# A two-layer hybrid encoder on one core: column tiles placed around a two-way scan, and the convolution branch's norm issued at other places

## The chip, the cores and the metric

The kernel runs on one core of one Trainium2 chip. The metric is the device time of one execution in microseconds (us), lower is better. Five engines work side by side, each through its own list of instructions in order, and wait for each other on semaphores: TensorE (PE in the profile) multiplies matrices, VectorE (DVE) and GpSimd (POOL) do elementwise work, ScalarE (ACT) does functions of one input and roundings, SyncE (SP) issues the weight transfers.

## What is computed

Two layers, 256 tokens, width 1024, all in float32. In each, with the gated branches in the middle:

```python
x = x + 0.5 * swiglu(rms_norm(x, norm_ffn1[i]), ffn1_w1[i], ffn1_w3[i], ffn1_w2[i])
h = rms_norm(x, norm_mix[i])
proj = h @ w_in[i]
y_rw, v_first = rwkv7_branch(p_rw, h, ...)       # a delta-rule scan over time, in both directions
y_cv = conformer_conv_branch(p_cv, ...)          # 31 taps, layer norm, silu, @ cv_w_branch
y_mla = mla_branch(p_mla, ...)                   # attention
merged = gates[:, :, 0] * y_rw + gates[:, :, 1] * y_cv + gates[:, :, 2] * y_mla
x = x + merged @ w_o[i]
x = x + 0.5 * swiglu(rms_norm(x, norm_ffn2[i]), ffn2_w1[i], ffn2_w3[i], ffn2_w2[i])
```

The end of the scan branch is a group norm over each head's 64 channels, and a bonus term:

```python
o = layer_norm(o, gn_g.reshape(H, N), gn_b.reshape(H, N), RW_GN_EPS)
k_bonus = jnp.mean(k_dir, axis=2).reshape(B, S, H, N)
bonus = jnp.sum(rf.reshape(B, S, H, N) * k_bonus * r_k, axis=-1, keepdims=True) * vf.reshape(B, S, H, N)
o = (o + bonus).reshape(B, S, C).astype(h.dtype)
return (o * g) @ w_branch, v_first
```

The convolution branch normalises over its 512 channels: `jax.nn.silu(layer_norm(u, ln_g, ln_b, CV_LN_EPS))`.

## The kernel before

Activations lie transposed, channels on the 128 partitions and the 256 tokens along them. **Column tiles.** The weights come as a stream of 128x1024 tiles, three slots deep. ACT rounds a tile to its high part (`hi`, L1108), DVE takes the rest (`lo`, L1443), and PE makes three products of each 128x128 block (`products`, L545 to L547: high weight times high and low activation, low weight times high activation). Three such products are a **piece**, and eight pieces are a tile (`tile_pieces`) or the two output tiles of a branch (`branch_pieces`). SP may refill a slot once the low part is taken; ACT may round into it once PE has used the tile before.

**The scan stage** follows the attention. It runs twice (`for d in range(2)`), once per direction, as a chain that hops between PE and DVE: decays and directed keys on DVE (`decays`, `directed`, then the products with the keys, L1820 to L1828), transposes on PE ("tk", L915), pair products for two quads of heads (`("pairs", d, q)`, L927 to L937, masked by DVE in L1842 to L1859), five levels of inverting a 64x64 triangle ("z", L948, and "mz", L957 and L959, with a DVE step after each), outputs (L997 to L1003), states and the sum `osum`. Then come the group norm: mean (L1061), bonus sums (L1064), squares summed (L1072), the inverse spread over the heads (L1077), and its elementwise end on DVE.

**Filling.** While PE waits in that chain it shall do column tiles. The tables `FILL_A` and `FILL_R` say how many pieces PE does at each named point of the chain (`fr.at("values")` and so on; one object per engine walks the same points). `FILL_R` hands out 192 pieces: 96 of the attention branch (weights and gates, which need its `u`), then 96 of the convolution branch, written by hand as counts and in this order only. ACT and DVE do one unit of their part (round the next tile, gate, merge into `merged`) at a point for each whole eight pieces that PE will have been given by then, so the same table moves work on three engines. The banks 6 and 7 take these pieces in turn, and a branch piece waits until DVE has merged what its bank held (`("merge", b, c)`). The scan branch's own tiles (`branch_pieces(2, ...)`) come last, after the group norm; they begin with two gate tiles and then need `u` of the scan.

**The convolution branch's norm** is threaded through the change of direction: PE sums the channels (`"cv mean"`, L1011), ACT scales, POOL subtracts (L508), ACT squares (L1402), PE sums (`"cv var"`, L1043), ACT takes the root (L1408), DVE the reciprocal (L1921), POOL multiplies (L515), ACT gives sigmoid and weighted value (L1372, L1375), POOL multiplies them (L520), ACT rounds (L1379), POOL takes the rest (L526), and PE's first convolution piece waits for that.

## Time and profile before

| what | value |
| --- | --- |
| three runs before | 1731.34, 1732.7, 1738.39 us, median 1732.7 |
| the profiled execution | 1740.08 us |
| its span, first to last instruction | 1738.1 us |
| PE's mean granted clock in it | 0.964 of 2.4 GHz |
| PE busy | 93% of the span |
| DVE busy | 69% |
| ACT busy | 45% |

The span is one execution seen by the profiler; 2.0 us of its time lie around it. A PE that is busy for 93% is not a PE at its peak: matmul ends are modelled, and at the lower of its two clocks (1.2 instead of 2.4 GHz) the same matmul counts as busy for longer. So the time of a stage is read from where a matmul starts, what it waited for, and the granted clock there.

### The profile page before, as it was taken

Reading aid. Unit: us, or ns where it says so; the run is one execution under the profiler, and the core shown is the slowest. Engines: PE = TensorE matmul, PEld = TensorE weight load, DVE = VectorE, ACT = ScalarE, POOL = GpSimd, SP = SyncE. Lnnn points to the kernel's source line nnn. Section 1 sums busy time; section 2 is a strip of 40 time slices with the busy share of each in tenths; the row PEclk is TensorE's granted clock in tenths of the full one; section 3 lists DMA queues with packets and bytes.
Section 4 is the critical chain, followed back from the end, with each engine's and each line's share of the span. In section 5 each row is a group of like instructions: output and inputs, shape, how many; then the busy total and the mean of one; then the engine's idle time right before and its main releaser. Section 6 shows DMA issues by size and latency. Waiting matters only on the chain.

```text
span 1738.1 us, 43046 instructions
## 1 busy us (share of the span) xinstructions
PE 1608.8 (93%) x16861; PEld 1489.9 (86%) x16861; DVE 1203.0 (69%) x1784; ACT 778.3 (45%) x1195; POOL 94.7 (5%) x112
## 2 busy tenths in 40 slices
PE   6999999898978899999999999988999798999998
PEld 6999886778868789999889999867788686899997
DVE  4777675788675456777666786667887655667766
ACT  5444564472251245544444446534614412454444
POOL 1000020000020001000100002000000200010001
PEclk9999998999999999999999999989999898999999
DMA  5755531331021234555557555322311202445555
GB/s 184 270 183 183 182 122 61 98 100 61 27 74 39 87 102 161 190 182 181 191 182 243 182 185 175 103 74 85 110 39 39 82 21 85 144 151 195 182 183 193
DMA packets 62925, 231.55 MB, mean 133 GB/s; under 512 B 7024, under 2 KB 8048, under 8 KB 61840
## 3 DMA queue, kind: packets, MB, share of 16 engines
q1 hardware_dynamic: 61488, 221.41, 38.7%
q0 software_dynamic: 1248, 7.46, 1.2%
q8 instruction: 138, 2.26, 0.5%
q14 instruction: 51, 0.42, 0.1%
HBM read 228.09 MB, written 1.05 MB: 132 GB/s over the span
## 4 chain that ended last, share of the span: by engine, by line
PE 79%; DVE 8%; issue 6%; ACT 4%; DMA 3%; POOL 0%; DVEq 0%; ACTq 0%; SPq 0%; POOLq 0%
PE banks L545 16%; PE banks L546 15%; PE banks L547 15%; PE banks L612 9%; PE banks L613 5%; DMA raw<-in_stream 3%; PE banks L959 2%; PE banks L957 2%; DVE wlo L1443 2%; PE banks L948 1%; ACT whi L1108 1%; DVE arena L1882 1%; PE banks L837 1%; ACT arena L1286 1%; PE banks L723 1%
## 5 line engine op out<-in xcount | busy, mean ns | idle before, releaser
L1443 DVE TENSOR_TENSOR wlo<-raw,whi 128x1024 fp32r<-128x1024 f32 x417 | 511.5, 1230 | 302.0 <-ACT whi L1108 300.1
L1108 ACT CAST whi<-raw 128x1024 fp32r<-128x1024 f32 x417 | 436.3, 1050 | 456.4 <-PE banks L547 315.3
L545 PE MATMUL banks<-hx,whi 128*128 128x256 f32 x1696 | 489.6, 289 | 39.8 <-DVE wlo L1443 18.7
L546 PE MATMUL banks<-hx,whi 128*128 128x256 f32 x1696 | 485.1, 286 | 0.0
L547 PE MATMUL banks<-hx,wlo 128*128 128x256 f32 x1696 | 484.8, 286 | 0.0
L545 PEld LDWEIGHTS banks<-hx,whi 128*128 128x128 f32 x1696 | 330.6, 195 | 45.1 <-issue 32.3
L546 PEld LDWEIGHTS banks<-hx,whi 128*128 128x128 f32 x1696 | 330.8, 195 | 0.2
L547 PEld LDWEIGHTS banks<-hx,wlo 128*128 128x128 f32 x1696 | 330.7, 195 | 0.0
L545 PE MATMUL banks<-h,whi 128*128 128x256 f32 x896 | 272.4, 304 | 29.4 <-ACT arena L1206 17.6
L546 PE MATMUL banks<-h,whi 128*128 128x256 f32 x896 | 261.3, 292 | 0.0
L547 PE MATMUL banks<-h,wlo 128*128 128x256 f32 x896 | 260.4, 291 | 0.0
L612 PE MATMUL banks<-gg,whi 128*128 128x512 f32 x704 | 245.8, 393 | 0.0
L545 PEld LDWEIGHTS banks<-h,whi 128*128 128x128 f32 x896 | 180.0, 201 | 48.1 <-issue 32.4
L613 PE MATMUL banks<-gg,wlo 128*128 128x256 f32 x704 | 197.3, 280 | 0.0
L546 PEld LDWEIGHTS banks<-h,whi 128*128 128x128 f32 x896 | 180.1, 201 | 0.7 <-issue 0.5
L547 PEld LDWEIGHTS banks<-h,wlo 128*128 128x128 f32 x896 | 179.5, 200 | 0.0
L612 PEld LDWEIGHTS banks<-gg,whi 128*128 128x128 f32 x704 | 132.5, 188 | 30.3
L613 PEld LDWEIGHTS banks<-gg,wlo 128*128 128x128 f32 x704 | 131.8, 187 | 0.0
L1671 DVE SCALAR_TENSOR_TENSOR cvx<-arena,vec_t,cvx 128x256 f32<-128x256 f32 x240 | 99.0, 479 | 0.0
L959 PE MATMUL banks<-arena 64*64 64x64 f32 x1280 | 72.5, 220 | 0.1
L959 PEld LDWEIGHTS banks<-arena 64*64 64x64 f32 x1280 | 69.8, 137 | 0.2
L1385 ACT COPY arena<-banks 128x512 f32<-128x512 f32 x8 | 4.7, 586 | 141.8 <-PE banks L966 141.8
(291 smaller groups left out, 1869.3 us busy)
## 6 DMA issues: line engine op xcount, KB each, us to landing
raw<-in_stream SPq DMA_DIRECT2D x417, 512.0 KB, 3.4
arena<-in_wuq POOLq DMA_DIRECT2D x2, 1152.0 KB, 10.3
lo_w<-in_lora POOLq DMA_DIRECT2D x2, 1024.0 KB, 7.0
arena<-in_wukv POOLq DMA_DIRECT2D x2, 1024.0 KB, 13.5
xT<-in_x SPq DMA_DIRECT2D x1, 1024.0 KB, 5.0
out<-xT SPq DMA_DIRECT2D x8, 128.0 KB, 3.7
consts<-in_cst SPq DMA_DIRECT2D x1, 642.5 KB, 8.4
vec_t<-in_vecs POOLq DMA_DIRECT2D x3, 113.0 KB, 4.1
```

Of the source, the lines that this page charges most:

```text
L545: TE.matmul(o, wh, hi, start=first, stop=False, **kw)
L546: TE.matmul(o, wh, lo, start=False, stop=False, **kw)
L547: return TE.matmul(o, wl, hi, start=False, stop=last, **kw)
L612: TE.matmul(o[:, :], whi[:, slot, w], gg[:, j, :, :], start=j == 0, stop=False, skip_group_check=True)
L613: last = TE.matmul(o[:, 0:S], wlo[:, slot, w], gg[:, j, 0, :], start=False, stop=j == NFF - 1, skip_group_check=True)
L723: m = TE.matmul(bank[4 + j // 2][:, (j % 2) * S:(j % 2 + 1) * S], wuq[:, c, j * P:(j + 1) * P], lat[:, c, :], start=c == 0, stop=c == QC - 1)
L837: m = TE.matmul(bank[two_banks[c // 2]][:, (c % 2) * S:(c % 2 + 1) * S], lo_w[HD * d:HD * d + HD, col, c * P:(c + 1) * P], wag[HD * d:HD * ...
L957: TE.matmul(bank[3 * q + 1][e, o], mn[e, 1, 4 * q + x, t, :], zz[e, 4 * q + x, t, :], start=True, stop=True)
L959: m = TE.matmul(bank[3 * q + 2][e, o], zz[e, 4 * q + x, t, :], mn[e, 1, 4 * q + x, t, :], start=True, stop=True)
L1108: SE.copy(whi[:, m % HL, :], raw[:, m % RAW, :]).then_inc(hi_ready, 1)
L1443: TT(wlo[:, m % HL, :], raw[:, m % RAW, :], whi[:, m % HL, :].bitcast(F), ALU.subtract)\
L1671: m = STT(cvo[:, c, :], src, vv("cv_w", c * TAPS + t), cvo[:, c, :], ALU.mult, ALU.add)
```

## The change

The table gives other counts, and two new points: "sums over" after the last sum of the scan, with 8 pieces, and "gn sums" after the group norm's squares, with 12. The sum stays 192. "values" gets 13 for 5, and the second direction's points before its levels get fewer. Around it the order on the engines moves: "cv mean" comes later on PE, "cv var" sooner, ACT's squares and DVE's reciprocal sooner; the sigmoid of the normalised values goes ahead of ACT's copies of the transposes; the sum of the directed keys and the bonus terms go from DVE's chain into the levels 3 and 4 of the second direction; a copy of 16 elements (`wch`) goes from DVE to ACT; the bonus sums take banks 4 and 5, since 6 and 7 hold pieces now.

```diff
-FILL_R = {"key sums": 6, "decay": 8, "nu": 5, "values": 5}
+FILL_R = {"key sums": 6, "decay": 8, "nu": 5, "values": 13}
 for _d in range(2):
-    FILL_R.update({("kr", _d): (14, 16)[_d], ("tk", _d): (4, 6)[_d], ("pairs", _d, 0): (6, 20)[_d],
-                   ("pairs", _d, 1): (6, 20)[_d], ("x", _d): (4, 18)[_d], ("o", _d): (4, 14)[_d]})
-    FILL_R.update({("state", _d, i): n for i, n in enumerate(((4, 4, 4), (12, 6, 6))[_d])})
+    FILL_R.update({("kr", _d): (14, 10)[_d], ("tk", _d): (4, 4)[_d], ("pairs", _d, 0): (5, 12)[_d],
+                   ("pairs", _d, 1): (6, 10)[_d], ("x", _d): (4, 16)[_d], ("o", _d): (3, 15)[_d]})
+    FILL_R.update({("state", _d, i): n for i, n in enumerate(((4, 4, 4), (12, 7, 6))[_d])})
+FILL_R.update({"sums over": 8, "gn sums": 12})
...
                 local(d, 1)
-                if d == 0:
-                    pe.wait_ge(*vec.at(("conv", *CONV_TAPS[-1][::-1])))
-                    for c in range(RC):
-                        m = TE.matmul(bank[5][:, 0:S], cc("ones", P), cvo[:, c, :], start=c == 0, stop=c == RC - 1)
-                    m.then_inc(*ten.mark("cv mean"))
                 fr.at(("o", d))
...
                 local(d, 2)
                 if d == 0:
+                    pe.wait_ge(*vec.at(("conv", *CONV_TAPS[-1][::-1])))
+                    for c in range(RC):
+                        m = TE.matmul(bank[5][:, 0:S], cc("ones", P), cvo[:, c, :], start=c == 0, stop=c == RC - 1)
+                    m.then_inc(*ten.mark("cv mean"))
                     lora(1, 0, (1, 4))
...
                     if d == 0 and i == 1:
                         pe.wait_ge(*act.at(("sw", 1)))
                         lora(1, 1, (1, 4))
+                        pe.wait_ge(*act.at("cv squares"))
+                        for c in range(RC):
+                            m = TE.matmul(bank[5][:, 0:S], cc("ones", P), cv_sq[:, c, :], start=c == 0,
+                                          stop=c == RC - 1)
+                        m.then_inc(*ten.mark("cv var"))
                 fr.at(("state", d, 2))
-                if d == 0:
-                    pe.wait_ge(*act.at("cv squares"))
-                    pe.wait_ge(*vec.at(("qw", d, 0)))
-                    for c in range(RC):
-                        m = TE.matmul(bank[0][:, 0:S], cc("ones", P), cv_sq[:, c, :], start=c == 0, stop=c == RC - 1)
-                    m.then_inc(*ten.mark("cv var"))
...
+            fr.at("sums over")
             pe.wait_ge(*vec.at(("osum", 1)))
-            pe.wait_ge(*vec.at("bonus terms"))
             for b in range(2):
                 m = TE.matmul(bank[b][:, :], cc("mean64", P), osum[:, 2 * b:2 * b + 2, :], start=True, stop=True)
             m.then_inc(*ten.mark("gn mean"))
+            pe.wait_ge(*vec.at("bonus terms"))
             for b in range(2):
-                m = TE.matmul(bank[6 + b][:, :], cc("mean64", P), tA[:, 2 * b:2 * b + 2, :], start=True, stop=True)
+                m = TE.matmul(bank[4 + b][:, :], cc("mean64", P), kds[:, 2 * b:2 * b + 2, :], start=True, stop=True)
             m.then_inc(*ten.mark("bonus"))
...
-                m = TE.matmul(bank[4][0:H, 0:S], cc("es", H, j * SUMS), tB[:, j, :], start=j == 0, stop=j == RC - 1)
+                m = TE.matmul(bank[0][0:H, 0:S], cc("es", H, j * SUMS), tB[:, j, :], start=j == 0, stop=j == RC - 1)
             m.then_inc(*ten.mark("gn sums"))
+            fr.at("gn sums")
             pe.wait_ge(*vec.at("gn inverse"))
...
                 SE.activation(tC_, tC_, ACT.Exp, scale=DECAY).then_inc(*act.mark(("winv", d)))
+                if d:
+                    sc.wait_ge(*vec.at(("qw", 0, 2)))
+                edge = C - 1 if d == 0 else 0
+                SE.copy(wch, tA.rearrange("p c (n e) -> p c n e", e=C)[:, :, :, edge]).then_inc(*act.mark(("wch", d)))
                 SE.preload_act_table(ACT.Sigmoid)
...
                 fr.at(("kr", d))
+                if d:
+                    for c in range(RC):
+                        sc.wait_ge(*poo.at(("cv normed", c)))
+                        SE.activation(cv_sq[:, c, :], cvo[:, c, :], ACT.Sigmoid, bias=vv("ln_b", c), scale=vv("ln_g", c))\
+                            .then_inc(*act.mark(("cv sigmoid", c)))
+                        if c % 2:
+                            for i in (c - 1, c):
+                                sc.wait_ge(*act.at(("cv sigmoid", i)))
+                                SE.activation(cvo[:, i, :], cvo[:, i, :], ACT.Identity, bias=vv("ln_b", i),
+                                              scale=vv("ln_g", i)).then_inc(*act.mark(("cv weighted", i)))
                 for q in range(6):
                     sc.wait_ge(*ten.at(("tk", d, q)))
                     SE.copy(tk[:, q // NT, q % NT, :], bank[q][:, :]).then_inc(*act.mark(("tk", d, q)))
                 fr.at(("tk", d))
                 if d:
-                    for c in range(RC):
...
                 fr.at(("x", d))
+                fr.at(("o", d))
                 if d == 0:
                     sc.wait_ge(*ten.at("cv mean"))
                     SE.mul(cv_st[:, 0, :], bank[5][:, 0:S], 1.0 / CV).then_inc(*act.mark("cv mean"))
-                fr.at(("o", d))
                 if d == 0:
                     sw(1, (1, 4))
+                    sc.wait_ge(*poo.at(("cv centred", RC - 1)))
+                    SE.activation(cv_sq, cvo, ACT.Square).then_inc(*act.mark("cv squares"))
                 fr.at(("state", d, 0))
                 if d == 0:
                     icl(1, (1, 4))
-                    sc.wait_ge(*poo.at(("cv centred", RC - 1)))
-                    SE.activation(cv_sq, cvo, ACT.Square).then_inc(*act.mark("cv squares"))
                 fr.at(("state", d, 1))
-                fr.at(("state", d, 2))
                 if d == 0:
...
                     SE.preload_act_table(ACT.Sqrt)
                     sc.wait_ge(*ten.at("cv var"))
-                    SE.activation(cv_st[:, 1, :], bank[0][:, 0:S], ACT.Sqrt, bias=cc("eps", 1, 2), scale=1.0 / CV)\
+                    SE.activation(cv_st[:, 1, :], bank[5][:, 0:S], ACT.Sqrt, bias=cc("eps", 1, 2), scale=1.0 / CV)\
                         .then_inc(*act.mark("cv rms"))
+                fr.at(("state", d, 2))
+            fr.at("sums over")
             sc.wait_ge(*vec.at("gn centred"))
             SE.activation(tB, osum, ACT.Square).then_inc(*act.mark("gn squares"))
+            SE.preload_act_table(ACT.Sqrt)
             sc.wait_ge(*ten.at("gn sums"))
...
                 .then_inc(*act.mark("gn rms"))
+            SE.preload_act_table(ACT.Sigmoid)
+            fr.at("gn sums")
...
-            SE.preload_act_table(ACT.Sigmoid)
...
+            def products_kk(d):
+                ve.wait_ge(*act.at(("wx", d)))
+                TT(kr_kk, by_tile(kk), by_tile(tD), ALU.mult).then_inc(*vec.mark(("kr kk", d)))
+
...
                 ve.wait_ge(*act.at(("icl", d)))
@@ -1791,12 +1810,10 @@
                     m = TS(kt[:, c, :], tB[:, c, :], -1.0, vv("k_a", c), ALU.add, ALU.mult)
                 m.then_inc(*vec.mark(("ka", d)))
                 ve.wait_ge(*vec.at(("ka", d)))
-                STT(kt, kt, 1.0, k_, ALU.add, ALU.mult).then_inc(*vec.mark(("kdir", d)))
-                ve.wait_ge(*vec.at(("kdir", d)))
-                if d == 0:
-                    V.tensor_copy(kds, kt).then_inc(*vec.mark("kds 0"))
-                else:
-                    TT(kds, kds, kt, ALU.add).then_inc(*vec.mark("kds 1"))
+                if d:
+                    products_kk(d)
+                    ve.wait_ge(*vec.at(("kr kk", d)))
+                STT(kdir(d), kt, 1.0, k_, ALU.add, ALU.mult).then_inc(*vec.mark(("kdir", d)))
...
-                ve.wait_ge(*act.at(("wx", d)))
-                TT(kr_kk, by_tile(kk), by_tile(tD), ALU.mult).then_inc(*vec.mark(("kr kk", d)))
+                if d == 0:
+                    products_kk(d)
...
-                TT(kt, kt, tC_, ALU.mult).then_inc(*vec.mark(("kt", d)))
+                TT(kt, kdir(d), tC_, ALU.mult).then_inc(*vec.mark(("kt", d)))
                 ve.wait_ge(*act.at(("w", d)))
-                edge = C - 1 if d == 0 else 0
-                V.tensor_copy(wch, tA.rearrange("p c (n e) -> p c n e", e=C)[:, :, :, edge]).then_inc(*vec.mark(("wch", d)))
...
+                    elif lv == 3:
+                        TT(kds, kds, kk, ALU.add).then_inc(*vec.mark("kds"))
+                    elif lv == 4:
+                        ve.wait_ge(*vec.at("kds"))
+                        for c in range(RC):
+                            m = STT(kds[:, c, :], kds[:, c, :], vv("r_k", c), r_[:, c, :], ALU.mult, ALU.mult)
+                        m.then_inc(*vec.mark("bonus terms"))
...
-                ve.wait_ge(*vec.at(("wch", d)))
+                ve.wait_ge(*act.at(("wch", d)))
...
                 if d == 0:
-                    directed(1)
                     ve.wait_ge(*act.at("cv rms"))
                     V.reciprocal(cv_st[:, 1, :], cv_st[:, 1, :]).then_inc(*vec.mark("cv inverse"))
+                    directed(1)
                 ve.wait_ge(*ten.at(("inter", d)))
...
-            for c in range(RC):
-                m = STT(tA[:, c, :], kds[:, c, :], vv("r_k", c), r_[:, c, :], ALU.mult, ALU.mult)
-            m.then_inc(*vec.mark("bonus terms"))
+            fr.at("sums over")
             ve.wait_ge(*ten.at("gn mean"))
...
-                m = STT(tC_[:, 2 * b:2 * b + 2, :], bank[6 + b][:, :].rearrange("p (c t) -> p c t", c=2), 0.5 * HD,
...
+                m = STT(tC_[:, 2 * b:2 * b + 2, :], bank[4 + b][:, :].rearrange("p (c t) -> p c t", c=2), 0.5 * HD,
...
             ve.wait_ge(*act.at("gn rms"))
             V.reciprocal(rn_rw[0:H, 1, :], rn_rw[0:H, 1, :]).then_inc(*vec.mark("gn inverse"))
+            fr.at("gn sums")
             ve.wait_ge(*ten.at("gn spread"))
```

In this kernel's order DVE does these instructions where the first direction ends (`L1443` rounds a tile, `L1789` to `L1799` are `directed(1)`, `L1921` is the convolution norm's reciprocal, `L1927` the first direction's `osum`, `L1820` to `L1828` the products with the keys; bookkeeping rows are left out):

```order
L1443 TENSOR_TENSOR wlo<-raw,whi 128x1024
L1789 TENSOR_TENSOR arena<-arena 128x1024
L1791 TENSOR_SCALAR arena<-arena,vec_t 128x256 x4
L1794 SCALAR_TENSOR_TENSOR arena<-arena 128x1024
L1799 TENSOR_TENSOR arena<-arena 128x1024
L1921 RECIPROCAL arena<-arena 128x256
L1927 TENSOR_TENSOR arena<-arena,banks 128x2x192 x2
L1820 TENSOR_TENSOR arena<-arena 128x8x128
L1823 TENSOR_TENSOR arena<-arena 128x1024
L1824 TENSOR_TENSOR arena<-arena 128x1024
L1827 COPY arena<-arena 128x16
L1828 TENSOR_TENSOR arena<-arena 128x8x128
```

And in the changed one (`L1454` rounds, `L1942` is the reciprocal, `L1808`, `L1810` and `L1816` `directed(1)`, `L1799` the product with the keys that PE's first transposes need, `L1949` `osum`, `L1840` to `L1843` the other products):

```order
L1454 TENSOR_TENSOR wlo<-raw,whi 128x1024
L1942 RECIPROCAL arena<-arena 128x256
L1808 TENSOR_TENSOR arena<-arena 128x1024
L1810 TENSOR_SCALAR arena<-arena,vec_t 128x256 x4
L1799 TENSOR_TENSOR arena<-arena 128x8x128
L1816 SCALAR_TENSOR_TENSOR arena<-arena 128x1024
L1949 TENSOR_TENSOR arena<-arena,banks 128x2x192 x2
L1840 TENSOR_TENSOR arena<-arena 128x1024
L1841 TENSOR_TENSOR arena<-arena 128x1024
L1843 TENSOR_TENSOR arena<-arena 128x8x128
```

The reciprocal went ahead of `directed(1)`, the sum of the keys and the small copy are gone from here, and `osum` now stands behind the product with the keys.

On PE, from the last state products of the scan (`L1052`) on, the order was (the matmuls of a piece repeat and are shown once):

```order
L1052 MATMUL banks<-arena 64x64 x24
L1061 MATMUL banks<-arena,consts 128x512 x2
L1064 MATMUL banks<-arena,consts 128x512 x2
L1067 MATMUL banks<-arena,lo_w 128x256 x4
L1072 MATMUL banks<-arena,consts 8x256 x4
L1077 MATMUL banks<-arena,consts 64x256 x8
```

and is now:

```order
L1051 MATMUL banks<-arena 64x64 x24
L546 MATMUL banks<-hx,whi 128x256
...
L546 MATMUL banks<-h,whi 128x256
...
L1060 MATMUL banks<-arena,consts 128x512 x2
L1064 MATMUL banks<-arena,consts 128x512 x2
L1067 MATMUL banks<-arena,lo_w 128x256 x4
L1072 MATMUL banks<-arena,consts 8x256 x4
L546 MATMUL banks<-h,whi 128x256
...
L1078 MATMUL banks<-arena,consts 64x256 x8
```

Eight pieces came in front of the group norm's mean, and twelve between its sums and the spread of its inverse.

## Rows read from the trace of the kernel before

**Rows 1.** Busy time by stretches of the first layer (columns in the first line)

```profile
core 0: us, PE busy (x) PEld busy (x) DVE busy (x) ACT busy (x) POOL busy (x), PEclk, DMA share, GB/s
419.00:420.00 1.00, 1.00 (x25) 1.00 (x22) 0.94 (x2) 0.00 (x0) 0.00 (x0) 0.50 0.00 0
422.00:454.00 32.00, 29.83 (x954) 28.87 (x948) 26.56 (x46) 2.94 (x5) 0.00 (x0) 1.00 0.02 4
531.00:566.00 35.00, 31.30 (x1010) 30.34 (x1007) 20.62 (x23) 2.82 (x5) 0.00 (x0) 1.00 0.06 19
548.00:549.00 1.00, 1.00 (x42) 1.00 (x40) 0.87 (x1) 0.00 (x0) 0.00 (x0) 1.00 0.00 0
600.00:611.00 11.00, 7.80 (x16) 3.93 (x16) 5.72 (x11) 2.34 (x2) 0.00 (x0) 0.69 0.15 48
628.00:655.00 27.00, 27.00 (x227) 27.00 (x226) 17.34 (x23) 11.51 (x16) 0.00 (x0) 1.00 0.61 196
```

**Rows 2.** Timeline of PE: start, length, engine, line, [idle before <-releaser]

```profile
392.11 0.43 PE L895 MATMUL banks<-consts,arena 128*128 128x128 f32 x2 [3.77 <-DVE arena L1815]
...
480.56 0.27 PE L1052 MATMUL banks<-arena 64*64 64x64 f32 x2
...
489.64 0.32 PE L915 MATMUL banks<-consts,arena 128*128 128x128 f32 x1 [1.51 <-DVE arena L1820]
...
495.89 0.34 PE L927 MATMUL banks<-arena 64*64 64x128 f32 x4
...
506.67 0.58 PE L545 MATMUL banks<-hx,whi 128*128 128x256 f32 x1 [8.34 <-POOL hx L526]
...
515.31 0.34 PE L927 MATMUL banks<-arena 64*64 64x128 f32 x4
...
532.43 0.28 PE L957 MATMUL banks<-arena 64*64 64x64 f32 x2 [1.35 <-DVE arena L1867]
...
603.20 1.22 PE L1061 MATMUL banks<-arena,consts 128*128 128x512 f32 x1 [3.64 <-DVE arena L1932]
...
615.42 1.54 PE L1077 MATMUL banks<-arena,consts 8*64 8x256 f32 x6 [2.33 <-DVE arena L1946]
...
626.27 0.28 PE L545 MATMUL banks<-hx,whi 128*128 128x256 f32 x1
...
1366.75 0.57 PE L545 MATMUL banks<-hx,whi 128*128 128x256 f32 x1 [8.34 <-POOL hx L526]
```

**Rows 3.** Timeline of DVE where the first direction ends

```profile
480.72 1.22 DVE L1789 TENSOR_TENSOR arena<-arena 128x1024 f32<-128x1024 f32 x1
...
485.43 1.75 DVE L1921 RECIPROCAL arena<-arena 128x256 f32<-128x256 f32 x1
...
487.09 0.95 DVE L1927 TENSOR_TENSOR arena<-arena,banks 128x384 f32<-128x384 f32 x2
...
487.96 1.37 DVE L1820 TENSOR_TENSOR arena<-arena 128x1024 f32<-128x1024 f32 x1
...
489.25 1.75 DVE L1823 TENSOR_TENSOR arena<-arena 128x1024 f32<-128x1024 f32 x1
...
490.92 1.75 DVE L1824 TENSOR_TENSOR arena<-arena 128x1024 f32<-128x1024 f32 x1
```

**Rows 4.** Timeline of POOL: the convolution branch's last steps

```profile
487.50 5.75 POOL L515 TENSOR_TENSOR cvx<-cvx,arena 128x256 f32<-128x256 f32 x4 [19.25 <-DVE arena L1921]
...
502.70 3.75 POOL L526 TENSOR_TENSOR hx<-cvx,hx 128x256 fp32r<-128x256 f32 x4
```

**Rows 5.** Groups by line: count, busy us, mean ns, idle before

```profile
L1443 DVE TENSOR_TENSOR wlo<-raw,whi 128x1024 fp32r<-128x1024 f32 x417 | 511.5, 1230 | 302.0 <-ACT whi L1108 300.1
...
L1108 ACT CAST whi<-raw 128x1024 fp32r<-128x1024 f32 x417 | 436.3, 1050 | 456.4 <-PE banks L547 315.3 <-PE banks L613 110.8 <-DMA raw<-in_stream 30.1
...
L1650 DVE TENSOR_TENSOR arena<-arena,gs 128x256 f32<-128x256 f32 x32 | 13.6, 425 | 1.1
...
L1375 ACT ACTIVATE cvx<-cvx,vec_t 128x256 f32<-128x256 f32 x8 | 4.8, 601 | 0.3
```

10 lines of the change are left out of this document (3 added, 7 removed).

## The prediction

> **What bounds the kernel now.** I first read the stretches [rows 1]. In 628 to 655 PE issues 227 matmuls in 27.00 us, one per 0.119 us at a granted clock of 1.00: PE is the bound there, and a piece of three costs 0.36 us. So only three things can be won: time in which PE waits, time at the lower clock, and nothing else, since the change leaves PE's matmuls as they are. Then I read PE's timeline [rows 2] for waits. Per layer the large ones are 3.77 us before the transposes of the values (DVE's L1815 is late), 1.51 us at the second direction's transposes, 8.34 us for the convolution branch's last POOL step, 3.64 us for the bonus terms and 2.33 us for the group norm's inverse. The 8.34 stands in the second layer too (1366.75), 860.08 us after the first: whatever holds per layer counts twice. Behind such waits the clock falls: 0.69 in 600 to 611 [rows 1].
>
> The DVE timeline [rows 3] shows why POOL is late: the reciprocal (485.43) stands behind `directed(1)` (from 480.72), POOL multiplies from 487.50 in 5.75 us, and its last step runs at 502.70 for 3.75 us [rows 4].
>
> **The change, by checkpoints in the first layer.** I walk PE's order; a checkpoint is a time and the count of pieces done by then. DVE rounds in 1.23 us, ACT in 1.05, a merge step takes DVE 0.42, a normalising step ACT 0.60 [rows 5].
>
> *Values.* Eight more pieces are 2.86 us inside the wait of 3.77 [rows 2]. The rounding of a tile (1.23) comes ahead of `directed(0)` on DVE, and a copy of the keys goes from behind it, so the first transposes slip by 0.6 or less. That is taken back before the levels: at quad 0 DVE has one rounding and one merge less (1.65). The first direction's levels start as before, with seven pieces banked.
>
> *End of the first direction.* Before: state products at 480.56 [rows 2], 74 pieces. Now 80 pieces are done by then, and the sums of the convolution norm only change places. The banked pieces cost nothing here; one piece less and a sum that no longer runs right behind a wait give up to 1.4 us. I take 479.2, with 480.6 as the other end, which would put all that follows 1.3 us later.
>
> *Second direction's transposes.* DVE's chain decides. Rounding unit 10 asks for PE's 80th piece, the last of its point, where the same place asked for the 72nd of 74. PE ends that piece at about 479.3, ACT rounds to 480.4, DVE to 481.6; before, DVE was free at 480.72 [rows 3]. Then come the reciprocal, 1.75, and `directed(1)`. POOL now multiplies beside it, from 483.3, so the DVE steps with two operands in SBUF take not 1.22 but 1.75, as L1823 did beside POOL [rows 3, 4]. b 1.7, ka 1.1, key product 1.75, keys 1.75, `osum` 0.95: 490.4, and PE starts 0.3 later, at **490.7 for 489.64**, 90 pieces in both. PE has six pieces less here and stands idle for 6 us, up from 1.51. That is the change's largest new wait. bt and kt meet POOL's next step and take 1.75 each [rows 3], so the last transposes start at 493.9. With four pieces instead of six the pairs of quad 0 start at **496.3 for 495.89, 94 pieces for 96**. Up to here the change has gained nothing: it has moved PE's idle time from the values to this place.
>
> *Quad 0 to quad 1.* The reciprocal is ready 3.9 us sooner. ACT makes eight normalising steps of 0.60 ahead of its copies, to about 492.2; POOL's product follows; rounding and POOL's 3.75 [rows 4] end at 500.2 instead of 506.45. PE arrives at 499.4 to 500.7: **of the 8.34 about 1 us is left.** But a convolution piece in bank 7 needs the merge of the attention branch's last column, which before stood ahead of the masks of quad 0 on DVE and now stands behind all five of them. By size, from 1.22 for 1024 columns [rows 3], they are two of 1.22, two of 0.7 for 512 columns and one of 1.3: 5.2 us from 498.2 or 499.3, when the pair products are there, then 0.42. So after four convolution pieces PE waits until 504.2 to 505.2, a new wait of 3. Six pieces more, and quad 1 starts at **506.4 to 508.2 for 515.31 [rows 2], 106 pieces for 116**. The later ends hold if PE runs at 1.2 GHz behind its 6 us wait.
>
> *To the levels.* Masks 5.2 us after the pair products' first two groups, one merge and one rounding (2.1), one mask 0.7: the first "mz" is at **516.4 to 518.1 for 532.43, 116 pieces for 136**.
>
> A rule speaks against this stretch. Before, in 490 to 498, PE ran three groups of transposes and pieces with no wait above 1.51 us before them; no row shows transposes behind a wait of 6 us. *The Trainium skill, "TensorE: Matmul & The Clock Gate", Part 4, says that a transpose does not count as busy PE in the way a matmul does. By it the clock would still be low when the four pieces and the pairs come, and 518.1 would hold rather than 516.4; no row here can tell.*
>
> *Levels.* From here both kernels do 56 pieces and the same matmuls until the scan's end. The keys' sum (1.22) in level 3 and the bonus terms (four of about 0.42) in level 4 cost between nothing and their whole 2.9; DVE is busy for 20.62 of 35 us there [rows 1], and both stand where it waits for PE, so I take 0.2, and 0.1 for a bank wait. The end of the scan comes 14.0 to 15.7 us sooner, at 583.8 to 585.5 for 599.5.
>
> *Behind the scan.* Call its end T. Before, T was 599.56 (603.20 less the wait of 3.64), and the scan branch's first weight product started at 626.27 [rows 2]: 26.7 us, with two waits of 5.97 together and no piece of the 192. From 603.20 to the next wait (613.09) PE took 9.89 for mean, bonus, gate product and squares' sum, and from 615.42 to 626.27 it took 10.85 for the spread and sixteen gate pieces, both with the clock down [rows 1, 2]. Each is 64 passes of 256 columns (a float32 matmul counts four, the spread's eight count two), so 7.6 at 0.119. Now: 8 pieces 2.9, 7.6, 12 pieces 4.3, which cover the wait of 2.33, and 7.6. That is 22.4; at worst, with the clock down as before, 28. DVE starts its end 0.9 us late because of the 24th unit, so the weights wait for `u`: I add 0.8. **T + 23.2, 3.5 less.** With no wait at T the clock has no cause to fall; before, it fell behind the 3.64.
>
> The sum is −(14.0 to 15.7) − 3.5 = −17.5 to −19.2 per layer, −35 to −38.4 for both. What I can't price (instruction gaps at other places, POOL and DVE meeting once more) can only be paid by these gains, so I take the near end, **−35**: 1740.1 becomes 1705.1 in the profiled execution, which was 7.4 us above the median, so the median becomes **1698**.
>
> **The rivals.**
> *A: the forecast*, 1690 to 1708.
> *B: the squeeze costs twice.* The 6 us wait, the late merge and the low clock behind each add 4 to 8 us per layer over my walk. For it: DVE has no idle time between 480 and 494 [rows 3], and each slip of it is one of PE. Against it: the 8.34 is gone in any case. −19 to −27: 1708 to 1724 (0.5% below the median is 1724).
> *C: no squeeze.* POOL and DVE do not collide (1.22 for 1.75), the clock stays at 1.00: 3 to 5 us per layer more, 1680 to 1690.
> *D: nothing moves.* If the convolution branch were late by as much as before, PE would wait until 506.7 with 98 instead of 96 pieces done, quad 1 would start 3.5 us sooner with ten pieces less, which is no gain; the tail's 3.5 and the banked pieces would remain. With two collisions as in B it is within 0.5%, 1724 to 1741. Against it stands the chain from the reciprocal, which has no step that it waits 6 us for.
> *E: slower, by the clock.* Twenty dense 128x128 pieces stood ahead of the levels at each quad; now ten or twelve do, and waits lie around them. If the levels then ran at 1.2 GHz: small matmuls issue at 25 per us at clock 0.50 and 42 at 1.00 (419 to 420, 548 to 549) [rows 1]. 1010 of them cost 40 us instead of 24, and some 430 more up to the scan's end 7 more: +23 per layer against −18, +10 in all, 1743 to 1750. It decides once more than 18/0.4 = 45 us of matmul work per layer fall to the lower clock. Against it: in the first direction the levels began at clock 0.50 behind six pieces and waits, and 422 to 454 ran at 1.00 [rows 1].
>
> **How the numbers follow.** A 0.57, B 0.24, C 0.08, D 0.07, E 0.04. The bound of faster and slower is 0.5%, 8.7 us, about what a measurement can tell here: faster is A, B and C, 0.89; same is D, 0.07; slower E, 0.04. The range takes A, and of B and C until two in ten are left out, with the bounds of the clock: 1684 to 1718.
>
> **What would show it.** Right: PE waits about 6 us before the second direction's transposes, about 1 for POOL, about 3 for a merge (the line of the last add into `merged`); no wait before the group norm's mean and below 0.5 before the spread; clock 1.00 behind the scan; both layers alike. Wrong: a wait above 4 us for POOL, or above 8 at the transposes (then B or D); a granted clock below 0.9 in the levels (E); the first "mz" less than 12 us sooner than 532.43; a wait for `u` above 2 us at the scan branch's weights.

## The result and the profile after

The changed kernel takes 1703.96 us (median of four runs, 1699.02 to 1706.5) where the kernel before took 1732.02 beside it: a ratio of 0.9831, 95% interval 0.9804 to 0.9858. The profiled execution took 1703.58 us, its span is 1701.9, the mean granted clock 0.976. The profiled spans differ by 36.2 us, the medians by 28.1. That of before was 8 us above its median. 4.2 of the 36.2 lie outside the stage that was changed (from the spread of the keys' norm, PE's L888, L887 in the code of before, to the scan branch's first weight product): 1.9 us ahead of the first layer's and 2.3 between the two. Within the stage the first layer takes 224.25 us for 241.86, the second 227.45 for 241.83: **17.6 and 14.4 us less, not twice the same.**

Busy time of PE by stretches of the first layer after the change, against [rows 1]:

```profile
core 0: us, PE busy (x) PEld busy (x) DVE busy (x) ACT busy (x) POOL busy (x), PEclk, DMA share, GB/s
457.00:470.00 13.00, 12.41 (x155) 10.80 (x156) 4.52 (x8) 0.26 (x1) 0.00 (x0) 0.61 0.13 43
483.00:493.00 10.00, 3.73 (x31) 3.53 (x31) 9.84 (x12) 9.93 (x16) 5.26 (x6) 0.85 0.16 53
519.00:552.00 33.00, 30.50 (x1007) 30.05 (x1008) 22.37 (x27) 2.53 (x5) 0.00 (x0) 1.00 0.07 20
584.00:595.00 11.00, 11.00 (x72) 7.34 (x67) 4.99 (x8) 3.75 (x4) 0.00 (x0) 1.00 0.29 97
595.00:607.00 12.00, 12.00 (x101) 11.02 (x100) 11.12 (x22) 5.33 (x10) 0.00 (x0) 1.00 0.27 89
```

The levels run at 1.00 as before. Behind the scan (584 to 607) PE is busy all the time at 1.00, where [rows 1] had 7.80 of 11 at 0.69. The idle time now lies in 483 to 493, in front of the second direction's transposes, where both DVE and ACT are busy throughout. And there is a stretch that the prediction did not price: 457 to 470 at 0.61.

PE's timeline at the same places as [rows 2] (start, length, line, [idle before <-releaser]):

```profile
390.48 0.39 PE L546 MATMUL banks<-hx,whi 128*128 128x256 f32 x1 [2.23 <-DVE arena L1657]
...
481.30 0.91 PE L1051 MATMUL banks<-arena 64*64 64x64 f32 x24
...
492.97 4.72 PE L916 MATMUL banks<-consts,arena 128*128 128x128 f32 x24 [6.27 <-DVE arena L1949]
...
501.42 0.39 PE L546 MATMUL banks<-h,whi 128*128 128x256 f32 x1
...
506.29 0.38 PE L546 MATMUL banks<-hx,whi 128*128 128x256 f32 x1 [2.45 <-DVE arena L1657]
...
519.66 0.34 PE L958 MATMUL banks<-arena 64*64 64x64 f32 x4 [1.30 <-DVE arena L1882]
...
587.45 0.59 PE L1060 MATMUL banks<-arena,consts 128*128 128x512 f32 x1
...
606.77 0.28 PE L546 MATMUL banks<-hx,whi 128*128 128x256 f32 x1
```

The wait of 8.34 us for POOL is gone, the values' wait of 3.77 is 2.23 and for another step, 6.27 stands before the transposes and 2.45 for the merge (L1657), and there is none behind the scan. The first "mz" is at 519.66 for 532.43. A wait of before that neither [rows 2] nor the prediction names is gone too. There the pieces of quad 1 waited for a merge (the last add into `merged`) behind the five masks:

```profile
523.01 0.43 PE L545 MATMUL banks<-hx,whi 128*128 128x256 f32 x1 [2.19 <-DVE arena L1650]
```

So the wait of 2.45 at quad 0 isn't an addition: it stands for one of 2.19 at quad 1.

DVE's and POOL's timelines between the two directions, against [rows 3, 4]:

```profile
482.49 1.23 DVE L1454 TENSOR_TENSOR wlo<-raw,whi 128x1024 fp32r<-128x1024 f32 x1 [1.56 <-ACT whi L1109]
483.63 1.75 DVE L1942 RECIPROCAL arena<-arena 128x256 f32<-128x256 f32 x1
485.29 1.16 DVE L1808 TENSOR_TENSOR arena<-arena 128x1024 f32<-128x1024 f32 x1
486.37 3.01 DVE L1810 TENSOR_SCALAR arena<-arena,vec_t 128x256 f32<-128x256 f32 x4
489.50 1.23 DVE L1799 TENSOR_TENSOR arena<-arena 128x1024 f32<-128x1024 f32 x1
490.76 1.22 DVE L1816 SCALAR_TENSOR_TENSOR arena<-arena 128x1024 f32<-128x1024 f32 x1
491.91 1.01 DVE L1949 TENSOR_TENSOR arena<-arena,banks 128x384 f32<-128x384 f32 x2
...
494.27 1.75 DVE L1841 TENSOR_TENSOR arena<-arena 128x1024 f32<-128x1024 f32 x1
```

```profile
485.71 3.52 POOL L516 TENSOR_TENSOR cvx<-cvx,arena 128x256 f32<-128x256 f32 x4 [12.60 <-DVE arena L1942]
491.26 5.34 POOL L521 TENSOR_TENSOR cvx<-cvx 128x256 f32<-128x256 f32 x4 [2.03 <-ACT cvx L1378]
498.92 2.88 POOL L527 TENSOR_TENSOR hx<-cvx,hx 128x256 fp32r<-128x256 f32 x4 [2.32 <-ACT hx L1387]
```

From 482.49 to 492.92 the chain on DVE has no gap above 0.12 us, and PE waits for its last step. Inside it the four `ka` steps (L1810) take 3.01 us. POOL's last step ends at 501.80 instead of 506.45.

The two stretches of a layer that the experiments compare are named here once: **R**, from the first direction's state products (L1051) to the scan branch's first weight product, and within it the tail, from the scan's end. R went from 145.7 and 145.6 us (before, both layers) to 125.47 and 125.46; the tail from 26.7 and 26.9 to 22.2. What lies ahead of R went from 96.15 and 96.24 us to 98.78 and 101.99. So the whole gain, some 20 us per layer, is in R, and up to 5.75 us of it is lost again ahead of it. Some 2.1 of the 20 are only moved: 80 of the 192 pieces are done ahead of R for 74, and six pieces are 2.1 us of PE. R also scatters within one program: it was 121.07 to 123.54 us in the four layers seen of unit10_later below, so a single difference under 2 us says little. Times "behind the start" are counted from the start of the stage.

### The profile page after: what moved, and what is told of

Read it like the earlier page. It is cut to its first block, busy times and chain, and to the rows that moved or that the text cites. A ratio compares the mean times of both kernels' runs of the same rounds, so it can differ in the third digit from the quotient of the medians.

```text
span 1701.9 us, 43044 instructions
## 1 busy us (share of the span) xinstructions
PE 1592.8 (94%) x16861; PEld 1479.1 (87%) x16861; DVE 1202.2 (71%) x1778; ACT 776.7 (46%) x1199; POOL 93.5 (5%) x112
## 4 chain that ended last, share of the span: by engine, by line
PE 77%; DVE 8%; issue 6%; ACT 4%; DMA 4%; DVEq 0%; ACTq 0%; SPq 0%; POOLq 0%
PE banks L546 15%; PE banks L548 14%; PE banks L547 14%; PE banks L613 10%; PE banks L614 5%; DMA raw<-in_stream 3%; PE banks L960 2%; DVE wlo L1454 2%; PE banks L958 2%; ACT whi L1109 1%; DVE arena L1904 1%; PE banks L949 1%; PE banks L916 1%; PE banks L838 1%; ACT arena L1287 1%
## 5 line engine op out<-in xcount | busy, mean ns | idle before, releaser
L1454 DVE TENSOR_TENSOR wlo<-raw,whi 128x1024 fp32r<-128x1024 f32 x417 | 511.4, 1230 | 289.2 <-ACT whi L1109 287.3
L546 PEld LDWEIGHTS banks<-hx,whi 128*128 128x128 f32 x1696 | 327.1, 193 | 35.6 <-issue 15.3
L547 PEld LDWEIGHTS banks<-hx,whi 128*128 128x128 f32 x1696 | 327.4, 193 | 0.2
L546 PE MATMUL banks<-h,whi 128*128 128x256 f32 x896 | 269.0, 300 | 31.9 <-ACT arena L1207 20.0
L547 PE MATMUL banks<-h,whi 128*128 128x256 f32 x896 | 258.2, 288 | 0.0
L546 PEld LDWEIGHTS banks<-h,whi 128*128 128x128 f32 x896 | 176.6, 197 | 51.9 <-issue 36.9
L547 PEld LDWEIGHTS banks<-h,whi 128*128 128x128 f32 x896 | 176.8, 197 | 0.5 <-issue 0.5
L960 PE MATMUL banks<-arena 64*64 64x64 f32 x1280 | 70.8, 218 | 1.7 <-issue 1.7
L960 PEld LDWEIGHTS banks<-arena 64*64 64x64 f32 x1280 | 68.9, 135 | 2.2 <-issue 1.8
```

The lines of the kernel that those rows point to most:

```text
L546: TE.matmul(o, wh, hi, start=first, stop=False, **kw)
L547: TE.matmul(o, wh, lo, start=False, stop=False, **kw)
L960: m = TE.matmul(bank[3 * q + 2][e, o], zz[e, 4 * q + x, t, :], mn[e, 1, 4 * q + x, t, :], start=True, stop=True)
L1454: TT(wlo[:, m % HL, :], raw[:, m % RAW, :], whi[:, m % HL, :].bitcast(F), ALU.subtract)\
```

## The experiments

Edits are against the changed kernel. "Low" is a granted clock of 0.50 to 0.78 in a slice of 4 us (1.00 is 2.4 GHz, 0.50 is 1.2).

**The order of the convolution norm alone.** The norm's mean, variance, reciprocal, sigmoid and weighting go back to their places in the code of before on PE, ACT and DVE; for instance

```
-                if d == 0:
-                    ve.wait_ge(*act.at("cv rms"))
-                    V.reciprocal(...)
                     directed(1)
+                    ve.wait_ge(*act.at("cv rms"))
+                    V.reciprocal(...)
```

> The changed kernel with the order of the convolution norm put back as before on all four places (mean ahead of the first direction's outputs, squares and variance behind the last state, reciprocal behind directed(1), sigmoid and weighting behind ACT's copies); all piece counts, the work behind the scan and the fused keys stay as changed. Theory (the two parts overlap: with only 12 + 10 pieces per quad instead of 20 + 20 the POOL chain is late again by its old time, and PE waits for it until about 506 to 507, but quad 1 then stands behind 10 pieces fewer): the wait for POOL at the second direction's first quad comes back with 5 to 7 us, the wait for the merge (2.45) goes, the transposes of the second direction wait about 4 us instead of 6.3; +2 to +3.5 us per layer against the change, ratio to the kernel before 0.986 to 0.988. Rival (the earlier convolution norm is most of the gain): the 8.3 us of wait come back whole, +6 to +8 us per layer, ratio 0.991 to 0.993. What it would also say: if it is no slower than the change, the reordering brings nothing by itself.

Measured: 1705.07 us, ratio 0.9855 (0.9829 to 0.9881). The waits of PE:

```profile
PE banks L546 <- POOL hx L527: 13.3, 2, 6.8
...
PE banks L916 <- DVE arena L1947: 6.6, 2, 3.3
```

(line: total us, times, longest). The wait for POOL is back with 6.8 us, the transposes wait 3.3 instead of 6.3, and R is 126.93 and 128.66 us: 1.5 and 3.2 more than after the change. The theory holds in the main: with the new counts the order is worth 1.5 to 3.2 us per layer in R, not 6 to 8. The wait for POOL is 6.80 and 6.47 us, but the wait before the transposes is 3.0 us shorter and the 2.45 for the merge are gone, which leaves 1.4 and 1.0. The rest of the second layer's 3.2 goes with the clock: between the transposes and the first "mz" its mean was 0.84 in the first layer and 0.76 in the second. The timed ratio is smaller than that for a reason that the theory didn't have: ahead of R this kernel stood at 94.98 and 96.35 us, 3.8 and 5.6 better than the change. In the whole time the earlier norm has therefore won nothing that can be told: the profiled span is 1699.2 us for the change's 1701.9, and the intervals of the ratios overlap (0.9829 to 0.9881, 0.9804 to 0.9858).

**The counts alone.** All counts as before, every move of the order kept:

```
-FILL_R = {"key sums": 6, "decay": 8, "nu": 5, "values": 13}
+FILL_R = {"key sums": 6, "decay": 8, "nu": 5, "values": 5}
...
-FILL_R.update({"sums over": 8, "gn sums": 12})
+FILL_R.update({"sums over": 0, "gn sums": 0})
```

> The changed kernel with the piece counts of before at every point (values 5, second direction 16/6/20/20/18/14/12/6/6, none behind the scan); every reordering stays. Theory: the convolution norm is ready before PE has done its 20 pieces at quad 0, so the wait of 8.3 us is gone by order alone, the 3.8 us wait at the values is back, and the waits behind the scan (3.6 for the bonus terms goes, as they are made in level 4; about 2.3 to 3 for the inverse stays): 7 to 8 us per layer of the gain stay and as many go, ratio to before 0.990 to 0.992. Rival 1 (the counts carry the gain, the order only allows them): ratio 0.995 to 1.0, with a new wait for the convolution pieces at bank 7 or for POOL above 3 us. Rival 2 (the counts are worth little): ratio below 0.986.

Measured: 1717.22 us, ratio 0.9924 (0.9900 to 0.9947). R is 137.57 and 137.45: 8.1 us of the 20.2 stay with the order alone, 12.1 belong to the counts. The time is the theory's 0.990 to 0.992 within the interval. One part of it was wrong, and there rival 1 had it: the wait at quad 0 isn't gone, 3.17 and 3.09 us of the 8.34 are left, and the transposes wait 3.72. The tail shows what the 20 pieces behind the scan are worth. Without them:

```profile
593.77 1.98 PE L1060 MATMUL banks<-arena,consts 128*128 128x512 f32 x4 [2.05 <-DVE arena L1949]
603.35 3.62 PE L1078 MATMUL banks<-arena,consts 8*64 8x256 f32 x16 [2.33 <-DVE arena L1966]
```

and with them, after the change:

```profile
587.45 1.88 PE L1060 MATMUL banks<-arena,consts 128*128 128x512 f32 x4
...
599.04 1.94 PE L1078 MATMUL banks<-arena,consts 8*64 8x256 f32 x16
```

The tail takes 22.52 us without any piece and 22.23 with 20. The pieces (7.2 us of PE) cover two waits of 4.38, and the sixteen spread matmuls take 1.94 instead of 3.62, since the clock no longer falls behind the wait (without the pieces it is at 0.50 from 605 to 609, gate pieces included). So 7.2 of the 12.1 us of the counts are made here, and 2.1 are the six pieces that are done ahead of R instead. Ahead of R old_counts stands at 93.33 and 95.63 us, 5.5 and 6.4 better than the change, so of the 12.1 the counts keep 6.7 and 5.6 over the whole stage.

**The eight early pieces.**

```
-FILL_R = {... "values": 13}
+FILL_R = {... "values": 5}
-    ("kr", _d): (14, 10)[_d]
+    ("kr", _d): (22, 10)[_d]
```

> The changed kernel with 5 pieces ahead of the values' transposes as before, and the 8 others given at the first direction's kr point (22 instead of 14), so that all later points see the same counts. The prediction took these 8 pieces as 2.9 us hidden under the 3.8 us wait. Theory from the trace of the changed kernel (the stretch has two new waits: 2.23 us for the merge that stands behind DVE's work at piece 29, and DVE waits 1.93 us for ACT's rounding ahead of directed(0)): the early pieces give almost nothing, within 1 us per layer either way, ratio to before 0.982 to 0.985. Rival (the sum of the prediction holds): the 3.8 us wait stands again in full and the 8 pieces cost 2.9 us behind it: +2.5 to +3 us per layer, +5.7 in all, ratio 0.9865.

Measured: 1701.24 us, ratio 0.9821 (0.9794 to 0.9848). The wait of 3.77 is back, the first pairs are 22.23 and 22.23 us behind the start (22.13 and 22.44 after the change), the first "z" 32.51 and 32.51 (32.41 and 32.72). The eight pieces at the values win nothing; the rival, which was the prediction's own sum, falls. R is 125.90 and 127.20 us; both kernels have done 80 pieces when it begins, so the second layer's 1.7 more is scatter as far as these runs show.

**The merge ahead of the masks.**

```
-    ("tk", _d): (4, 4)[_d], ("pairs", _d, 0): (5, 12)[_d],
+    ("tk", _d): (4, 6)[_d], ("pairs", _d, 0): (5, 10)[_d],
```

> The changed kernel with two pieces moved in the second direction from the first quad's point behind the masks to the point behind the transposes (tk 6 instead of 4, quad 1's point 10, quad 0's point 10 instead of 12), so that DVE rounds unit 12 and adds the merge of the attention branch's last column ahead of quad 0's masks. Theory (the wait of 2.45 us is for this merge alone, which stands behind five masks): it goes, quad 0's pairs start 0.7 us later, its masks 1 to 1.5 us later; net -1 to -2 us per layer, ratio to before 0.981 to 0.9825, first mz of the second direction 1 to 2 us sooner. Rival (the masks set quad 1 and the levels, and whatever stands ahead of them on DVE delays the level start by as much): 0 to +1.5 us per layer, ratio 0.983 to 0.985.

Measured: 1701.15 us, ratio 0.9832 (0.9803 to 0.9860). R is 124.67 and 125.06, 0.8 and 0.4 us less: neither the 1 to 2 of the theory nor the loss of the rival. The merge's wait is gone and a wait for POOL of 3.1 us stands in its place (6.2 in all, two times). In the changed kernel POOL was done at 501.80 and the merge only at 506.23, so POOL had 4.4 us to spare. The edit itself took them. The two pieces also move ACT's unit of that point (gate, rounding of the next tile), which now waits for PE's pieces ahead of the rounding that POOL's last step needs (L1387):

```profile
497.50 0.38 ACT L1229 ACTIVATE gs<-banks 128x256 f32<-128x256 f32 x1 [1.52 <-PE banks L548]
497.78 1.04 ACT L1109 CAST whi<-raw 128x1024 fp32r<-128x1024 f32 x1
498.72 1.32 ACT L1387 CAST hx<-cvx 128x256 fp32r<-128x256 f32 x4
```

This rounding starts 8.4 us behind the first transpose, for 5.3 in the changed kernel (498.25 against 492.97), and POOL ends 12.4 us behind it for 8.8. This kernel's layers also gave the clearest view of something else. The stretches from 60 to 76 and from 76 to 92 us behind the start, in its first and its second layer:

```profile
444.04:460.04 16.00, 14.24 (x512) 13.62 (x509) 15.27 (x34) 4.86 (x8) 0.00 (x0) 1.00 0.02 4
460.04:476.04 16.00, 16.00 (x207) 13.83 (x203) 6.81 (x14) 6.95 (x13) 2.80 (x4) 1.00 0.16 50
```

```profile
1280.24:1296.24 16.00, 15.51 (x537) 14.93 (x537) 14.92 (x33) 4.85 (x8) 0.00 (x0) 1.00 0.02 5
1296.24:1312.24 16.00, 14.25 (x207) 12.41 (x197) 5.36 (x10) 0.38 (x1) 0.91 (x2) 0.68 0.11 35
```

The code is the same in both layers. In the second one the clock is at 0.68 behind the sparse products of the outputs, and the state products come 102.09 us behind the start instead of 94.63. It is the drop of 457 to 470 in the changed kernel's profile.

**The mean sum as a dense block at that place.**

```
                 local(d, 1)
+                if d == 0:
+                    pe.wait_ge(*vec.at(("conv", *CONV_TAPS[-1][::-1])))
+                    for c in range(RC):
+                        m = TE.matmul(bank[5][:, 0:S], cc("ones", P), cvo[:, c, :], ...)
+                    m.then_inc(*ten.mark("cv mean"))
                 fr.at(("o", d))
```

(and these lines away from their place ahead of `lora(1, 0, (1, 4))`)

> The changed kernel with the mean sum of the convolution norm (8 matmuls of 256 columns) back ahead of the first direction's outputs; nothing else moved. Theory (behind the sparse products of the outputs and PE's gap of 1.2 to 1.8 us there, TensorE is at 1.2 GHz for 8 to 14 us in most layers seen of the changed kernel, and 3 to 7 us are lost to it; dense sums at the place of the gap keep it at 2.4, as in cv_order_back, both of whose layers had 1.00 there): granted clock 1.00 in the stretch 76 to 92 us behind the stage's start in both layers, the first direction's state products (L1051) 95 to 97 us behind the start instead of 98.8 and 102.0, and 6 to 10 us less in the profiled execution: ratio to before 0.978 to 0.981. Rival 1 (the drop comes and goes by execution, whatever stands there): one or both layers still show 0.5 to 0.6 there, ratio 0.981 to 0.985. Rival 2 (the mean's wait for the last convolution tap on DVE now stands in PE's way): a new wait above 0.5 us at the mean sum, as large a loss as the gain.

> The changed kernel itself once more, on the chip of its neighbours. Every theory: ratio to before 0.980 to 0.986; 125 to 126 us per layer from the first direction's state products to the scan branch's first weight product. Theory of the clock as chance (one program, different by execution and layer): the state products stand 95 to 97 us behind the stage's start where the granted clock stays 1.00 behind the outputs and 98.5 to 102 where it falls; not both layers need be as in the first profile. Rival (it is fixed by the program's order): 98.8 and 102.0 again within 0.5.

Measured, on one chip: 1702.34 us, ratio 0.9798 (0.9776 to 0.9820), and the changed kernel itself 1705.44 us, ratio 0.9834 (0.9810 to 0.9858). The second layer of the one, then the first of the other, 76 to 92 us behind the start:

```profile
1300.58:1316.58 16.00, 14.57 (x346) 13.14 (x339) 7.49 (x16) 3.93 (x9) 2.79 (x4) 1.00 0.11 36
```

```profile
458.58:474.58 16.00, 14.66 (x190) 12.37 (x183) 5.27 (x10) 0.59 (x2) 1.83 (x3) 0.68 0.12 35
```

With the mean ahead both layers stay at 1.00; the changed kernel has the low clock in its first layer (state products at 101.42) and not in its second (97.07). So the drop comes and goes with one and the same program, and 98.8 and 102.0 aren't fixed by it, as the theory of chance said. Whether the mean's place also bears on it is for the count below. The first layer (94.73) came out just below the theory's 95 to 97. The second (98.47) lost 2.52 us in a gap at L960 in which PE waited for nothing that the profile shows.

**DVE's chain before the transposes, shortened by one rounding.**

```
-    ("kr", _d): (14, 10)[_d]
+    ("kr", _d): (14, 11)[_d]
-    enumerate(((4, 4, 4), (12, 7, 6))[_d])
+    enumerate(((4, 4, 3), (12, 7, 6))[_d])
```

> The changed kernel with one piece moved from the last point of the first direction (3 instead of 4) to the second direction's kr point (11), so that DVE rounds unit 10 of the weights behind the keys instead of ahead of the reciprocal. Theory (PE's wait of 6.3 us at the second direction's transposes is DVE's chain, and 1.56 + 1.23 us of it are this rounding and its wait for ACT): the wait falls to about 3.5 (PE has one piece more before it, 0.36), quad 0's pairs 2.5 us sooner; the POOL chain starts 2.8 us sooner too, so the waits at quad 0 do not grow: -2 to -2.8 us per layer from the state products to the scan branch's first weight product (125.5 in both layers of the change), ratio to before 0.980 to 0.982. Rival (the 1.2 us of rounding come back where they now stand, ahead of the merge for PE's bank 7 or of the masks): the wait at the transposes falls as said, and the wait for the merge grows from 2.45 to 4 or more: within 1 us per layer.

Measured: 1700.25 us, ratio 0.9790 (0.9772 to 0.9808). The transposes wait 3.41 us, R is 121.32 and 123.54: 4.2 and 1.9 less than the change, for the theory's 2 to 2.8. The rival falls, since the merge's wait didn't grow (1.46 and 2.35). The two layers differ by the clock: from the first transpose to the first "mz" they take 24.75 us at a mean of 0.94 and 26.12 at 0.89 (26.7 at 0.86 in the changed kernel's first). On the chip of after_again the intervals of the two kernels do not touch (0.9772 to 0.9808, 0.9810 to 0.9858).

**The reciprocal two steps later.**

```
                 m.then_inc(*vec.mark(("ka", d)))
+                if d:
+                    ve.wait_ge(*act.at("cv rms"))
+                    V.reciprocal(...)
```

> The changed kernel with the reciprocal of the convolution norm two steps later on DVE: behind b and ka of directed(1), ahead of the key products. Theory (the four tensor_scalar steps ka took 3.0 us in the change because POOL multiplied beside them, and would take about 1.15 alone): ka 1.15 us in all, the transposes of the second direction 1.5 to 1.9 us sooner (wait 4.5 instead of 6.3); POOL starts 2.3 us later and ends 1.5 to 2.3 later, which takes up some of the merge's wait of 2.45 as a wait for POOL: -0.5 to -1.9 us per layer. Rival 1 (ka is slow for its own sake in this place, as by ACT): ka stays at 3 us and all of it is later: 0 to +2 us per layer. Rival 2 (the collision goes with POOL to the key products and keys): these take 1.75 each instead of 1.22, and 0.8 to 1.1 us of the 1.9 are given back.

Measured: 1701.13 us, ratio 0.9799 (0.9772 to 0.9826). DVE's timeline:

```profile
486.80 1.22 DVE L1808 TENSOR_TENSOR arena<-arena 128x1024 f32<-128x1024 f32 x1
487.93 1.14 DVE L1810 TENSOR_SCALAR arena<-arena,vec_t 128x256 f32<-128x256 f32 x4
488.98 1.74 DVE L1814 RECIPROCAL arena<-arena 128x256 f32<-128x256 f32 x1
490.65 1.16 DVE L1799 TENSOR_TENSOR arena<-arena 128x1024 f32<-128x1024 f32 x1
491.84 1.63 DVE L1819 SCALAR_TENSOR_TENSOR arena<-arena 128x1024 f32<-128x1024 f32 x1
```

The four `ka` steps take 1.14 us without POOL beside them and took 3.01 with it. The keys now meet POOL and give 0.41 back (1.63 for 1.22). The transposes wait 4.58, R is 123.15 and 123.16: 2.3 us less per layer, a little more than the theory's 0.5 to 1.9. In the second layer PE now waits 0.45 us for POOL at quad 0; it falls into the time in which it waited for the merge (1.76 for 2.45).

**Together.** The first is the last two counts and the dense mean, the second adds the merge ahead of the masks, the third the late reciprocal:

```
both_a = unit10_later + mean_early
both_b = both_a + merge_first
both_c = both_b + recip_after_ka
```

> unit10_later and mean_early together. Theory (the two gains have nothing to do with each other: one is DVE's chain at the second direction's transposes, the other the granted clock behind the first direction's outputs): wait at the second direction's transposes 3.4 us, 121 to 124 us per layer from the first direction's state products to the scan branch's first weight product, and no layer at 0.50 in the stretch 76 to 92 us behind the stage's start; 2 to 5 us faster than unit10_again on the same chip, ratio to before 0.976 to 0.979. Rival (the clock's drop there is chance, and four layers without it so far with the mean ahead were luck): drops of 8 to 14 us at 0.50 to 0.78 here too, time within 2 us of unit10_again.

> both_a with merge_first (two pieces moved from quad 0's point to the one behind the transposes) on top. Theory (with the chain 2.5 us shorter, PE's two waits between quad 0 and quad 1 are 0.7 for POOL and 1.5 for the merge; moving the merge ahead of the masks turns them into one wait for POOL of 1 to 1.5): -0.5 to -1 us per layer against both_a, not to be told by the time alone, but by the waits. Rival (PE gains nothing, since POOL's last step sets when quad 1 starts): 0 within 0.5 us per layer, wait for POOL 2 us or more.

> both_b with recip_after_ka on top. Theory (POOL's chain now ends last at quad 0; 2.3 us of delay for its start minus the 1.9 that the ka steps win): the wait at the second direction's transposes falls to about 1.6, the wait for POOL at quad 0 grows to 3.5 to 4.5, no gain or a loss of up to 1 us per layer against both_b. Rival (DVE's chain is still the only bound, as recip_after_ka's -2.3 us per layer suggests): -1 to -2 us per layer against both_b, ratio to before 0.973 to 0.976.

> unit10_later once more beside the combinations. Every theory: wait of 3.4 at the second direction's transposes, ratio to before 0.977 to 0.982. Theory of the dense sum: each layer may show the low clock in the stretch 76 to 92 us behind the stage's start (6 of the 10 layers seen without the mean ahead did), and then its state products stand 2 to 5 us later. Rival: none here either, as in its first profile, and then the mean's place has nothing to do with it.

| kernel | median us | ratio (95%) | R, both layers | wait before the transposes |
|---|---|---|---|---|
| both_a | 1693.69 | 0.9760 (0.9729 to 0.9792) | 122.63, 121.08 | 3.42 |
| both_b | 1696.90 | 0.9780 (0.9751 to 0.9810) | 124.48, 124.10 | 3.42 |
| both_c | 1691.24 | 0.9746 (0.9720 to 0.9772) | 122.21, 122.83 | 1.68 |
| unit10_again | 1697.29 | 0.9793 (0.9764 to 0.9822) | 122.42, 121.07 | 3.42 |

unit10_again has the low clock behind the outputs in its second layer, so its rival (none here either) falls. both_c's transposes and its wait at quad 0, in the first layer:

```profile
487.20 1.09 PE L916 MATMUL banks<-consts,arena 128*128 128x128 f32 x8 [1.68 <-DVE arena L1951]
...
499.79 0.38 PE L546 MATMUL banks<-hx,whi 128*128 128x256 f32 x1 [3.43 <-DVE arena L1868]
```

both_c is faster than the changed kernel with intervals that don't touch (0.9720 to 0.9772 against 0.9810 to 0.9858), by about 15 us of 1732. Behind the dense mean and the shorter chain, both_b won nothing: its R is 2 to 3 us longer than both_a's, and both theory and rival missed that. One wait of 3.09 at quad 0 took the place of both_a's (2.32 in the first layer, 0.80 and 1.41 in the second). The profile puts it down to a mask of DVE, but POOL's last step ends 0.2 us ahead of the matmul (502.36, 502.58), 11.8 us behind the first transpose for 10.0 and 9.5 in both_a. The cause is the one of merge_first: ACT's unit waits 1.46 us for PE ahead of the rounding for POOL. Another 1.1 and 0.9 us lie between the first "mz" and the scan's end, where both_b has gaps of 0.85 and 0.58 in which PE waits for nothing shown, and both_a none. Against both_b the late reciprocal wins 2.3 and 1.3 us in R: there the rival was right, although the wait of 3.43 that the theory named is there too (the row names DVE, the second layer's of 3.44 POOL, which is done 0.2 us before in both). both_c still carries the moved unit of ACT; the late reciprocal on both_a, without it, was not run.

**The count of low clocks** in 76 to 92 us behind the start, one profiled execution of two layers for each kernel. With the mean behind the outputs and the changed kernel's counts (the change twice, values_5, merge_first, unit10_later twice, recip_after_ka): in 7 of 14 layers three slices in a row are low, and one more layer has a single one at 0.57. With the mean ahead of the outputs (cv_order_back, mean_early, both_a, both_b, both_c): in none of 10, and one layer has a single slice at 0.63. The kernel before, with the mean ahead too, has one slice at 0.67 and 0.69 in its layers, and old_counts one at 0.58 in one of two. Were the place of no matter, ten layers without a drop beside seven drops in fourteen would be rare (about one in a hundred). But that counts the layers that gave the idea: in the runs made after it was written down there are three drops in eight layers and none in eight, which chance gives once in ten, and two layers of one execution need not be independent. The times say the same twice, but weakly (1702.3 against 1705.4 and 1693.7 against 1697.3, intervals overlapping). So I hold it likely that the place of the dense sum bears on the drop, but these runs do not show it. Why the drop comes in one layer and not in the next of the same program stays open.

## Why the prediction was right, and where it was not

The forecast was 1698 in a range of 1684 to 1718, and faster with 0.89. It came to 1704, and both layers were to be alike, which they were not (17.6 and 14.4 us). Step by step, with times behind the stage's start (subtract 384.41 from the forecast's):

| | before | forecast | after, both layers |
|---|---|---|---|
| state products of direction 0 | 96.15 | 94.8 | 98.78, 101.99 |
| from there to the transposes | 9.1 | 11.5 | 11.7, 11.7 |
| wait before them | 1.51 | 6 | 6.27, 6.27 |
| wait for POOL at quad 0 | 8.34 | 1 | 0, 0 |
| wait for a merge | 2.19 (quad 1) | 3 (quad 0) | 2.45, 2.45 (quad 0) |
| from state products to the scan's end | 119.0 | 104.6 to 106.3 | 103.2, 103.2 |
| tail | 26.7 | 23.2 | 22.2, 22.2 |

**The sum was right in part by luck.** In the profile the stage had to come 35 us sooner for both layers, and came 32.0 sooner. The first direction lost 11.2 against the forecast; from there to the scan's end the layers won 3.1 each on the near end that the sum took, and 1.0 each in the tail. The median is 6.3 above the unrounded 1697.7 for reasons in which the stage has the smaller part: 3.0 from the stage; 4.5 the other way from outside it (4.2 in the span, 0.3 around it); and 7.8 from a term that nothing showed, that the changed kernel's profiled execution would lie 7.4 above its median as that of before did. It lay 0.4 below. The rivals' bounds don't follow from their own terms either: B's 4 to 8 us per layer more are 1706 to 1714 and not 1708 to 1724, C's 3 to 5 less are 1688 to 1692 and not 1680 to 1690.

**The end of the first direction failed**, the largest miss of a step. The prediction let a drop of the clock out, and a gap: it took 479.2 "with 480.6 as the other end", where the layers of the changed kernel stand 4.0 and 7.2 us later than 479.2, counted from the stage's start. Where neither drop nor gap came (the first layers of merge_first 94.63, mean_early 94.73, cv_order_back 94.98 and unit10_again 95.27) the 94.8 was right to 0.5 us. A drop costs 4 to 5 us (101.42 against 97.07 in the two layers of after_again, which have a gap at L960 both; 98.78 against 94.8 in the change's first layer, which has none). The gap, 1.7 to 2.5 us about 41 us behind the start in which PE waits for nothing that the profile shows, is in 19 of the 24 layers with the changed counts or nearly these, the change's second among them, and in none of the four of before and old_counts. The profile of before showed a low clock of 0.67 there too, in rows that the prediction did not read.

**"The banked pieces cost nothing here" was wrong in size.** Eight pieces at the values were 2.86 us inside a wait of 3.77. But PE's 29th piece waits 2.23 us for a merge on DVE (L1657) and DVE another 1.93 for ACT's rounding, so the values' transposes start 10.22 us behind the start instead of 7.70. values_5 shows that nothing is lost by giving them up. The seven pieces that are banked by the first "z" cost 1.5 us of their 2.5 (it starts 32.41 us behind the start for 30.93).

**The wait of 6 us was right, one term by another way.** The sum had 1.75 for the key product and the keys, beside POOL, and 1.1 for `ka`. It was the other way round: 1.23, 1.22 and 3.01, in all 0.86 more, and b 1.16 for 1.7. (The steps as the prediction lists them add up to 490.6 and not 490.4.) POOL's own steps took 3.52 and 2.88 us where [rows 4] had 5.75 and 3.75, but POOL waited 2.03 and 2.32 us for ACT between its steps. So it was done 20.5 us behind the state products, where the forecast had 21.0, and PE came to its first convolution piece at 20.9: that is why nothing was left of the wait.

**The low clock there held, its end did not.** In slices from the changed kernel:

```profile
493.00:495.00 2.00, 2.00 (x10) 2.00 (x11) 2.00 (x2) 1.15 (x4) 2.00 (x3) 0.50 0.00 0
495.00:497.00 2.00, 2.00 (x12) 2.00 (x11) 2.00 (x2) 1.47 (x3) 1.60 (x1) 0.53 0.00 0
497.00:499.00 2.00, 2.00 (x19) 1.91 (x17) 2.00 (x3) 1.98 (x6) 0.08 (x1) 1.00 0.00 0
499.00:501.00 2.00, 2.00 (x78) 1.95 (x80) 0.15 (x1) 0.58 (x2) 2.00 (x3) 1.00 0.35 90
```

The transposes run at 0.50 behind the wait for most of their time, but the four pieces and the pairs of quad 0 at 1.00. The first piece starts at 497.45 and the rise is before 497.00, while PE had done nothing but transposes since 492.97. The Trainium skill, "TensorE: Matmul & The Clock Gate", Part 4, says that a transpose doesn't count as busy PE in the way a matmul does; by what the prediction drew from it the clock would still have been low at the pieces, and the trace says otherwise. The clock then fell a second time, behind the wait of 2.45 for the merge, on most of the last six pieces and the first pairs of quad 1:

```profile
507.00:509.00 2.00, 2.00 (x12) 2.00 (x11) 0.37 (x1) 0.39 (x1) 0.00 (x0) 0.53 0.26 53
509.00:511.00 2.00, 2.00 (x36) 1.77 (x39) 1.23 (x1) 0.65 (x1) 0.00 (x0) 0.62 0.58 217
```

So the first "mz", 38.4 us behind the state products, is near the late end of the forecast (37.2 to 38.9), in part by a low clock at a place where the prediction had none. merge_first's first layer, which has no second fall, needed 37.6.

**The tail and the levels were a little better than summed.** The 0.8 us for `u` did not come, and the spread kept the clock. From the first "mz" to the scan's end the changed kernel took 64.9 us for 67.1, where the forecast had 67.4; of that, two gaps of before in which PE waited for nothing shown are 0.72 us (in the levels) and 1.61 (in the outputs), and the changed kernel has one of 0.78. Of the rivals, D is refuted by the wait of 0 for POOL and E by the levels at 1.00. B's place, from the wait of 6 us to the levels, came out as forecast; the loss that came was in the first direction, which B did not name. C had the key product and the keys right (1.23 and 1.22) but neither `ka` nor the clock.

## What to carry to other kernels

A wait that is filled with moved work is worth what the next chain leaves of it: here the earlier norm, aimed at a wait of 8.34 us, was worth 1.5 to 3.2 per layer in R beside the new counts and nothing clear in the whole time, and 20 pieces in the tail, with no late chain behind them, their full 7.2. Before such a move, ask of each engine what its last step is at that place and put nothing on it there: one rounding taken out of DVE's chain won 2 to 4 us per layer, and eight pieces put into a wait at the values won nothing. Where one table moves work on several engines, look at each of them: two pieces moved on PE cost POOL's chain 3.5 us, by ACT's unit that moved with them. And where one program gives two layers of different length, look at the granted clock of both before a mechanism is made of either; one profile of one layer would have priced this change 3 us wrong.

## What the hardware showed that was not expected

- Four TENSOR_SCALAR steps of 256 columns with one operand in SBUF took 3.01 us beside POOL's multiply and 1.14 without it, while the TENSOR_TENSOR of 1024 columns that POOL's step began beside took 1.16. The Trainium skill, "GPSIMD Engine Reference", section 1, says that GpSimd shares its SBUF interface with VectorE, and that they contend where a VectorE instruction runs in a two-port mode or has two inputs in SBUF. The steps with one input agree if they run in such a mode, which no row tells. Of those with two inputs L1841 agrees, 1.75 us beside POOL's L521, and b (L1808) doesn't, 1.16 us though POOL multiplied in more than half of them; nor do the keys (L1816), 1.22 us with POOL's L521 beside them from 491.26.
- Behind a wait of 1.68 us the transposes ran at 1.00 (eight in 1.09 us, both_c); behind 3.4 to 6.3 us part of them ran at 0.50.
- PE had a gap of 0.9 to 1.9 us that no engine explains, 74 to 80 us behind the start, in all 28 layers seen, and the second one at L960 that is counted above. What PE does in them stays open.
